# Forget block, attention keys, gates and branches computed by feature in a transformer block on one core

## What is computed

```python
h = rms_norm(x, pre_mix_norm[l])
proj = h @ w_in[l]
(hq, hf, hi, hg, mq, mk, mv, dq, dkv, iq, ik, iw, gates) = jnp.split(proj, splits, axis=-1)
y_a = hgrn2_mixer(hq, hf, hi, hg, lower_bounds[l], hg_norm_w[l])     # f = lb + (1-lb) sigmoid(hf)
y_b = moba_attention(mq, mk, mv, bias_b)
y_c = dsa_attention(dq, c_kv, w_uk, w_uv, iq, ik_n, iw, bias_c, n_keep)
g = jax.nn.sigmoid(gates.reshape(B, S, N_BRANCH, D_MODEL))
merged = (g[:, :, 0] * (y_a @ w_branch_a[l])
          + g[:, :, 1] * (y_b @ w_branch_b[l])
          + g[:, :, 2] * (y_c @ w_branch_c[l]))
x = x + rms_norm(merged @ w_out[l], post_mix_norm[l])
h2 = rms_norm(x, pre_ffn_norm[l])
gate, up = jnp.split(h2 @ w_ffn_in[l], 2, axis=-1)
x = x + rms_norm((jax.nn.silu(gate) * up) @ w_ffn_out[l], post_ffn_norm[l])
```

## Time and profile before

| | before |
|---|---|
| median of 3 runs | 463.78 us (463.74 to 463.91) |
| the profiled execution's own time | 463.29 us |
| its span, first to last instruction | 461.6 us |
| granted TensorE clock, share of full speed | 0.999 |
| TensorE busy | 454.1 us (98%), 3318 matmuls |
| VectorE busy | 301.5 us (65%) |
| ScalarE busy | 248.9 us (54%) |
| GpSimd busy | 49.1 us (11%) |

### The profile page before, as it was taken

One profiled execution on the slowest core, in us unless ns is written; L12 is line 12 of the kernel. 1 busy time (PEld: TensorE's weight loads), 2 busy tenths in 40 slices (PEclk: granted clock), 3 DMA queues, 4 the chain that ended last, 5 costly groups with the idle time before them and its releaser, 6 DMA issues.

```text
span 461.6 us, 8038 instructions
## 1 busy us (share of the span) xinstructions
PE 454.1 (98%) x3318; PEld 400.3 (87%) x3318; DVE 301.5 (65%) x403; ACT 248.9 (54%) x370; POOL 49.1 (11%) x50
## 2 busy tenths in 40 slices
PE   8999999999999999999999999999999999999994
PEld 7799798987788888888888888999999999888883
DVE  4657689898628746577449797866565665743532
ACT  5768369338485955526443462855544554433410
POOL 2301002456630100000000000100000000000000
PEclk9999999999999999999999999999999999999999
DMA  8997665545434464569565544666666656766202
GB/s 296 398 296 221 187 172 179 173 130 159 148 125 135 140 183 136 184 186 322 190 210 186 184 168 148 216 192 189 188 191 207 192 187 188 247 200 186 89 0 91
DMA packets 26024, 85.60 MB, mean 185 GB/s; under 512 B 3171, under 2 KB 4740, under 8 KB 25988
## 3 DMA queue, kind: packets, MB, share of 16 engines
q1 hardware_dynamic: 25268, 84.31, 57.4%
q10 hardware_dynamic: 720, 0.79, 0.5%
HBM read 83.84 MB, written 1.25 MB: 184 GB/s over the span
## 4 chain that ended last, share of the span: by engine, by line
PE 97%; DVE 1%; DMA 1%; SPq 0%; ACT 0%; issue 0%; DVEq 0%
PE bank L1450 56%; PE bank L1444 31%; PE bank L1476 1%; PE bank L1620 1%; PE bank L1485 1%; DMA raw<-w_stream 1%; PE bank L1632 1%; PE bank L1660 1%; PE bank L1604 1%; PE bank L1584 1%; PE bank L1575 1%; PE bank L1521 1%; PE bank L1523 0%; PE bank L1526 0%; PE bank L1633 0%; PE bank L1664 0%
## 5 line engine op out<-in xcount | busy, mean ns | idle before, releaser
L843 DVE TENSOR_TENSOR wl<-raw,wh 128x1024 fp32r<-128x1024 f32 (+1 forms) x150 | 185.0, 1267 | 44.3 <-ACT wh L514 44.0
L514 ACT ACTIVATE wh<-raw 128x1024 fp32r<-128x1024 f32 (+1 forms) x150 | 153.5, 1049 | 83.7 <-PE bank L1450 42.0
L1444 PE MATMUL bank<-hTh,wh 128*128 128x256 f32 x416 | 116.2, 279 | 0.0
L1444 PE MATMUL bank<-hTl,wh 128*128 128x256 f32 x416 | 115.1, 277 | 0.0
L1444 PE MATMUL bank<-hTh,wl 128*128 128x256 f32 x416 | 115.1, 277 | 0.0
L1450 PE MATMUL bank<-wh,hTh 128*128 128x512 f32 (+1 forms) x216 | 85.4, 395 | 0.2 <-DVE wl L843 0.2
L1450 PE MATMUL bank<-wh,hTl 128*128 128x512 f32 (+1 forms) x216 | 83.0, 384 | 0.0
L1450 PE MATMUL bank<-wl,hTh 128*128 128x512 f32 (+1 forms) x216 | 83.0, 384 | 0.0
L1444 PEld LDWEIGHTS bank<-hTh,wh 128*128 128x128 f32 x416 | 78.1, 188 | 0.5 <-issue 0.3
L1444 PEld LDWEIGHTS bank<-hTh,wl 128*128 128x128 f32 x416 | 78.2, 188 | 0.1
L1444 PEld LDWEIGHTS bank<-hTl,wh 128*128 128x128 f32 x416 | 78.2, 188 | 0.0
(11 more groups left out here) (227 smaller groups left out, 528.7 us busy)
## 6 DMA issues: line engine op xcount, KB each, us to landing
raw<-w_stream SPq DMA_DIRECT2D x146, 512.0 KB, 4.1
raw<-w_stream SPq DMA_DIRECT2D x4, 328.0 KB, 6.5
x<-x_in SPq DMA_DIRECT2D x4, 256.0 KB, 4.2
raw<-w_stream SPq DMA_DIRECT2D x4, 256.0 KB, 4.3
bias<-bias_scratch SPq DMA_DIRECT2D x8, 128.0 KB, 4.8
x<-x_in SPq DMA_DIRECT2D x1, 1024.0 KB, 5.7
out<-mo SPq DMA_DIRECT2D x3, 256.0 KB, 2.0
post<-post_mix ACTq DMA_DIRECT2D x1, 512.0 KB, 9.8
```

Of the source, the lines that this page charges most:

```text
L514: did(act.activation(wh[:, u % SPLIT, place(u)], raw[:, u % RING, place(u)], ACT.Copy), high_done, u + 1 - EARLY)
L843: did(dve.tensor_tensor(wl[:, u % RING, place(u)], raw[:, u % RING, place(u)], wh[:, u % SPLIT, place(u)].bitcast(F32), ALU.subtract), low ...
L1444: ins = pe.matmul(bank[bk][:, i * S:(i + 1) * S], w_[:, k, h * P:(h + 1) * P], x_[:, kt, :], start=first, stop=final, skip_group_check=True)
```

## The change

Fourteen blocks are made by feature in place of by token: `hf`, `mk`, the six gate and the six branch blocks. Their transposes (`hfT`, `mkT`, `mTa`, `mTb`) go. A new job `row1` makes the factors of the first norm a row, from `qp` (which holds ones at that time) and a diagonal that VectorE writes; ScalarE copies it to `row1`. `by_token` on VectorE multiplies PSUM by that row for `hf`, `mk` and the gates. ScalarE then applies its sigmoids in SBUF. `merged` is kept by feature, and its high and low halves (`mTh`, `mTl`) are written straight from it. `SHIFT` becomes 32 floats, 128 bytes, so all stationary units, those of the feed-forward layer too, move by 64 bytes in their slots.

```diff
 CHUNKS = DFF // 512
-BY_FEATURE = ("dq", "hq", "mq") + tuple(f"f{c}{j}" for c in "gu" for j in range(CHUNKS))
+BY_FEATURE = ("dq", "hf", "hq", "mq", "mk") + tuple(f"{n}{b}{c}" for n in ("gate", "branch") for b in BRANCHES for c in range(2)) + tuple(f"f{c}{j}" for c in "gu" for j in range(CHUNKS))
 SHIFTED = BY_FEATURE + ("uk",)
-SHIFT, PLACE = 16, 1024 + 64
+SHIFT, PLACE = 32, 1024 + 64
...
 N_MASKS = len(IN_STRIP) * HALF_STRIP
-JOBS = (["hT00", "hT10", "hT01", "hT11", "rel", "ckvT", "iqT0", "iqT1", "kc0", "kc1", "vc0", "vc1", "ikT"]
-        + [f"ix{i}" for i in range(6)] + ["hfT0", "hfT1",
+JOBS = (["hT00", "hT10", "hT01", "hT11", "rel", "ckvT", "iqT0", "iqT1", "row1", "kc0", "kc1", "vc0", "vc1", "ikT"]
+        + [f"ix{i}" for i in range(6)] + [
                                           "diag", "L1", "dl0", "dl1", "dl2", "L2", "L4", "L8", "L16",
-                                          "mkT0", "mkT1", "mkT2", "mkT3", "L32", "dP0", "dP1", "dP2", "dP3", "L64", "dO0", "dO1", "L128",
+                                          "L32", "dP0", "dP1", "dP2", "dP3", "L64", "dO0", "dO1", "L128",
                                           "ml0", "ml1", "ml2", "ho0", "ho1", "mP0", "mP1", "mP2", "mP3",
                                           "mO0", "mO1", "yaT0", "yaT1", "yaT2", "yaT3",
-                                          "mTa0", "mTa1", "mTa2", "mTa3", "mTb0", "mTb1", "mTb2", "mTb3", "h2T00", "h2T01", "h2T10", "h2T11",
+                                          "h2T00", "h2T01", "h2T10", "h2T11",
                                           "row", "fT"])
...
         sig = sb("sig", [P, 3, TT, 512])
-        skip = [sb("skip0", [P, SHIFT])]
+        row1 = sb("row1", [P, S])
+        skip = [sb("skip0", [P, 16])]
         yh = [sb(f"yh{b}", [P, H, S], F32R) for b in range(3)]
...
         iws = sb("iws", [P, TT, NI], stack=early)
-        skip.append(sb("skip1", [P, SHIFT], stack=early))
+        skip.append(sb("skip1", [P, 16], stack=early))
         ckvT = sb("ckvT", [P, RT, S], stack=early)
...
         row2 = row.rearrange("p (o s) -> p o s", o=1).to_broadcast([P, 2, S])
+        diag1 = prob[:, 0:S]
+        rows1 = row1[:].rearrange("p (o s) -> p o s", o=1).to_broadcast([P, 2, S])
+        merged2 = merged[:].rearrange("p t d -> p (t d)").rearrange("p (c t n) -> p c t n", c=2, t=TT)
...
             o_sums one_exp out_mean out_rstd out_squares out_sums prob_ready relu_used score_ready
-            silu_last silu_done row_diag fT_low fgu_high down_eps stored x1_ready x1_squares x_rstd x_squares y_high
+            silu_last silu_done row_diag row1_diag row1_ready gate_sig mT_low fT_low fgu_high down_eps stored x1_ready x1_squares x_rstd x_squares y_high
         """.split()
...
             copy_jobs(["iqT1"], lambda i: flat(iqT, 1))
+            ps = wait_job(act, "row1")
+            did(act.activation(row1[:], ps[:, 0:S], ACT.Copy), *job_read("row1"))
             high_until(17)
...
                 did(act.activation(relu[:, i % 2], ps[:, 0:512], ACT.Relu, scale=DI ** -0.5), *job_read(f"ix{i}"))
-            stage_copy("hf", 0, 512, 21)
-            high_until(22)
-
             high_until(24)
             for i in range(2):
-                ps = wait_job(act, f"hfT{i}")
-                did(act.activation(flat(pre, i), ps[:, 0:512], ACT.Sigmoid))
-                did(act.activation(flat(kT, i), ps[:, 0:512], ACT.Sigmoid, scale=-1.0), *job_read(f"hfT{i}"))
+                act.wait_ge(*block_read("hf", i))
+                did(act.activation(flat(pre, i), stage[:, 0, i], ACT.Sigmoid))
+                did(act.activation(flat(kT, i), stage[:, 0, i], ACT.Sigmoid, scale=-1.0))
             act.wait_ge(lb_ready, 1)
...
             normalise(0)
-            stage_copy("mk", 0, 512, LAST_UNIT["mk"] + 5)
-            high_until(40)
-            for r in range(NSTRIP):
-                ps = wait_job(act, f"mkT{r}")
-                did(act.activation(token_strip(kcT, r), strip_bank(ps), ACT.Copy), *job_read(f"mkT{r}"))
             high_until(41)
...
                 name = f"gate{b}{c}"
-                high_until(LAST_UNIT[name] + 4)
-                if c:
-                    after_block(act, f"branch{b}0")
+                high_until(LAST_UNIT[name] + 5)
                 for t in range(TT):
-                    ps = wait_block(act, name, t)
-                    did(act.activation(sig[:, b, t], ps[:, 0:512], ACT.Sigmoid, scale=stat(X_RS + t)), *block_read(name, t))
+                    act.wait_ge(*block_read(name, t))
+                    did(act.activation(sig[:, b, t], sig[:, b, t], ACT.Sigmoid), s["gate_sig"], TT * (3 * c + i) + t + 1)
...
             probT_copy("m")
-            gates(1, 0)
+            high_until(52)
             y_high(["mO0", "mO1"], 1, 1)
...
                 did(act.activation(token_strip(yh[0], r), strip_bank(ps), ACT.Copy), s["y_high"], 5 + r)
+            gates(1, 0)
             gates(2, 0)
             high_until(FIRST_UNIT[f"gate{BRANCHES[0]}1"] + 5)
+
             def m_high(c):
-                for r in range(NSTRIP):
-                    ps = wait_job(act, f"mT{'ab'[c]}{r}")
-                    did(act.activation(token_strip(mTh, r, 4 * c, 4), strip_bank(ps), ACT.Copy), s["mT_high"], 4 * c + r + 1)
+
+                for t in range(TT):
+                    act.wait_ge(s["merged"], 4 * c + TT + t + 1)
+                    did(act.activation(f_tiles(mTh, c, t), pair(merged2[:, c, t]), ACT.Copy), s["mT_high"], TT * c + t + 1)
...
                     s["ckv_ready"], t + 1)
+            for t in range(TT):
+                dve.wait_ge(eye_made, 1)
+                did(dve.tensor_scalar(diag1[:, t * P:(t + 1) * P], eye[:], stat(X_RS + t), None, ALU.mult), s["row1_diag"], t + 1)
             low_until(11)
...
+            def by_token(name, dst):
+
+                for t in range(TT):
+                    ps = wait_block(dve, name, t)
+                    did(dve.tensor_tensor(pair(dst(t)), pair(ps[:]), rows1, ALU.mult), *block_read(name, t))
+
             for i in range(6):
+                if i == 4:
+                    after_job(dve, "row1")
+                    by_token("hf", lambda t: stage[:, 0, t])
                 add_heads(i)
...
             low_until(37)
+            by_token("mk", lambda t: flat(kcT, t))
             level(4)
...
                         did(ins)
+            def gate_rows(i, c):
+
+                b = BRANCHES[i]
+                by_token(f"gate{b}{c}", lambda t: sig[:, b, t])
+
+            low_until(49)
+            gate_rows(0, 0)
             low_until(52)
+            gate_rows(1, 0)
             y_low(["mO0", "mO1"], 1, 1)
...
                     low_until(LAST_UNIT[f"branch{b}{c}"] + 3)
-                    after_block(dve, f"gate{b}{c}")
+                    dve.wait_ge(s["gate_sig"], TT * (3 * c + i + 1))
                     for t in range(TT):
                         ps = wait_block(dve, f"branch{b}{c}", t)
-                        dst = merged[:, t, c * 512:(c + 1) * 512]
+                        dst = merged2[:, c, t]
                         out_ = dst if i == 0 else tmp[:, t]
...
                         for t in range(TT):
-                            dst = merged[:, t, c * 512:(c + 1) * 512]
+                            dst = merged2[:, c, t]
                             n_merged[0] += 1
...
             def m_low(c):
-                for r in range(NSTRIP):
-                    ps = wait_job(dve, f"mT{'ab'[c]}{r}")
-                    dve.wait_ge(s["mT_high"], 4 * c + r + 1)
-                    did(dve.tensor_tensor(token_strip(mTl, r, 4 * c, 4), strip_bank(ps), token_strip(mTh, r, 4 * c, 4).bitcast(F32), ALU.subtract),
-                        *job_read(f"mT{'ab'[c]}{r}"))
-
+                for t in range(TT):
+                    dve.wait_ge(s["mT_high"], TT * c + t + 1)
+                    did(dve.tensor_tensor(f_tiles(mTl, c, t), pair(merged2[:, c, t]), f_tiles(mTh, c, t).bitcast(F32), ALU.subtract), s["mT_low"], TT * c + t + 1)
+
+            low_until(LAST_UNIT[f"gate{BRANCHES[2]}0"] + 4)
+            gate_rows(2, 0)
             merge(0)
...
             m_low(0)
+            for i in range(3):
+                low_until(LAST_UNIT[f"gate{BRANCHES[i]}1"] + 4)
+                gate_rows(i, 1)
             merge(1)
...
                             h = 2 * t + i
-                            for w_, x_ in ((rh, hTh), (rl, hTh), (rh, hTl)):
-                                first = kt == i == 0 and w_ is rh and x_ is hTh
-                                final = kt == n_kt - 1 and x_ is hTl
+                            for w_, x_ in ((rh, high), (rl, high), (rh, low)):
+                                first = kt == i == 0 and w_ is rh and x_ is high
+                                final = kt == n_kt - 1 and x_ is low
                                 ins = pe.matmul(bank[bk][:, i * S:(i + 1) * S], w_[:, k, h * P:(h + 1) * P], x_[:, kt, :], start=first, stop=final,
...
             transposes("iqT1", tiles(stage[:, 1], 0))
```

(21 more changed lines are left out.)

## The result

The changed kernel takes 472.06 us (median, 471.77 to 472.11) against 463.78 us before: ratio 1.0175, 95% interval 1.0164 to 1.0186. It is slower by 8.3 us, where 3.9 us less was forecast. The rival that the shift makes the slow pace the rule is what happened. Single executions far above the others of their kernel (925.12 us in e2, 504.85 in e13, 1610.17 in e14, 1174.98 and 1616.57 in the kernel before) are left out of all that follows.

What follows compares the result with a forecast made beforehand. The prediction took TensorE's own instruction stream as the bound: 463.29 us - 3.43 + 0.35 + 0 - 0.77 gave 459.4, as a median 459.9 us. The forecast's own range was 459.3 to 460.6, the wider range 459.2 to 463.2.

Steps and rivals of the forecast that it cites:

- The rival that the shift makes the slow pace the rule: Every by-feature unit: 0.11 us more for each slow one, 470.5 us with all 96 slow; chance 0.18.
- TensorE's stream is the time: Whole kernel: TensorE busy 98% of 461.6 us, 97% of the chain, its products waiting 0.2 us for a weight unit.
- Four transposition groups, 3.43 us, less row1's 0.35: TensorE loses the hfT, mkT, mTa and mTb transposes, 3.43 us, and gains the row1 product, 0.35 us.
- 528 matmuls turned into 1056 at no cost: hf, mk, gate and branch blocks: two by-feature matmuls at 113.3 ns cost one by-token at 226.7, so 0.
- Shifted: 64 to 128 bytes, "I take the fast end": All by-feature units at their new place: none slow any more, seven slow ones gained back, - 0.77 us.
- The other end: Same shift of the stationary units: all 96 by-feature units slow, 9.8 us more.
- The rival that the shift does nothing: By-feature units: slow ones stay and restarts are drawn as before, 461.4 us or 462.7 us; chance 0.20.
- VectorE and ScalarE moves at nothing: Norm multiplications for hf, mk and gates, and sigmoids in SBUF: covered by time to spare, cost 0.
- a late engine: Rival: VectorE or ScalarE late, the copy of the transposed probabilities first, 1 to 3 us back, 461 to 463; chance 0.07.

Runs made afterwards that it cites:

- e2: Kernel before with its stationary weights moved to 128 bytes, nothing else changed; 469.46, 471.4 and 471.63 us.
- e13: Changed kernel with the high halves of the weights at 64 bytes and the low halves at 192; 460.09 us, ratio 0.9912 to 0.9955.
- e14: Changed kernel with its stationary weights at 64 bytes and one gate unit alone at 192; 462.68 us, ratio to the kernel before 0.9987.
- e16: Kernel before with the high halves of the weights at 64 bytes and the low halves at 192; 463.04 us, ratio 0.9978 to 1.0001.
- e15: Changed kernel with high halves of the weights at 64 bytes and low halves at 192, a repeat of e13; 460.35 us, ratio 0.9929.
- e11: Kernel before with only its stationary weights moved to 128 bytes, a repeat of e2 for its profile; 469.65 us.
- e1: Changed kernel with its stationary weights back at 64 bytes, all else kept; 464.91 us, ratio to the kernel before 1.0024.
- e7: Changed kernel with its stationary weights at 64 bytes and the token operands also moved by 64 bytes; 479.16 us, ratio to the kernel before 1.0325.
- e9: Changed kernel with its stationary weights at 64 bytes, but at 192 from the third gate to the last branch; 464.95 us, ratio 1.0030.
- e10: Changed kernel with its stationary weights at 64 bytes in even units and at 192 in odd units; 461.62 us, ratio 0.9952.
- e12: Changed kernel with each by-feature unit's first k-tile at 64 bytes and its second at 192; 460.19 us, ratio 0.9941.

## Why the prediction was wrong, point by point

- *TensorE's stream is the time.* Right: 98% busy, the same chain, the same waits. The 0.2 us of waiting for weights left out the 0.3 us at the start, which both kernels have.
- *Four transposition groups, 3.43 us, less row1's 0.35.* Right. The pauses are gone, row1 costs 0.36, and e16 less e15 gives 2.7 for the net 3.1.
- *528 matmuls turned into 1056 at no cost.* Right at the held pace: 26 gate and branch units at 113.3 ns in e15, where before 226.7 was taken by token. The Trainium skill ("TensorE: Matmul & The Clock Gate", section "Back-to-back issue gap") gives N/2.4 + 2.5 ns as the gap of an isolated matmul, a condition that the prediction left out when it held the rule against a stream. The 2.5 ns show here as little as in the earlier trace rows.
- *Shifted: 64 to 128 bytes, "I take the fast end".* This step failed. Its ground was that 45 of 52 by-feature units were fast, but those were 45 units at 64 bytes, in few stretches that keep what they draw; they said nothing of 128 bytes. The other end, which the working had (all 96 slow), was the case, and even that was a little low: 118.7 to 120 ns instead of 117.9, 0.13 a unit instead of 0.11, so 472.06 instead of the rival's 470.5. The term was - 0.77 us; measured, it is 12.4 less 0.77, + 11.6. With that the sum is 463.29 - 3.08 + 11.6 = 471.8, and the profiled execution took 471.77. e11 shows that the shift alone does it: 6.1 us on the old kernel.
- *The rival that the shift does nothing* had its price too low. At 64 bytes (e1) the change has 464.9, not 461.4 to 462.7: 50 slow units, not 13 or 25. The long stretch from u51 on, which it named, did start slow, and the gate blocks ahead of it too. The prediction took from the Trainium skill ("SBUF — State Buffer", section "Who interferes with whom": two independent read ports, shared with nobody) that a place could not matter. The runs disagree: between e7 with 120.0 ns and e1 with 113.3 or 117.8 only the token operands, and the tensors behind them, were moved.
- *VectorE and ScalarE moves at nothing; a late engine.* Right: TensorE waits nowhere that it didn't wait in the kernel before. That holds in e15 too, where its products run at 113.3 ns and leave the other engines less time.

What stays open: why the distance between the two operands sets the pace, and whether it is their reads that disturb each other; why a restart begins fast or slow at 64 and 192 bytes (e1, e9 and e14 have the same places up to u49, and u49 runs at 118 ns in e1 and e14 and at 113 in e9); and why a step away and back moves a stretch to the fast pace while none was seen to move one to the slow pace. In e10, e12 and e14 no stretch turned at a step from 64 to 192. One step from 192 to 64 can be enough, as at u52 in e10, behind a unit that itself started at 192; it was not enough at u30 and u32. The runs show that it is so and not by what.

## What to carry to other kernels

A unit's address is part of its price: before taking a pace over to another place or another form, find a row at that place, and count stretches between pauses, not units, when judging how often a pace occurs. When a change moves the time by a few per cent and no engine waits, compare the start-to-start distance of the main matmul before and after in a block that the change was not meant to touch; here the feed-forward blocks told it in two rows. Where the stationary operand is the streamed one, letting its high and low parts lie 64 bytes to either side of the moving operand's place (modulo 256) gave 460.35 us against 463.04 for the old form with the same places and 463.58 for the kernel before.

## What the hardware showed that was not expected

- The pace of a 256-column matmul depends on the distance between weights and token columns modulo 256 bytes: 120.0 ns at 0, 118.7 (in places 120) at 128, 117.3 to 118.7 in the long stretches at 32 and 96, 113.3 or 117.8 at 64 and 192.
- A 512-column matmul with the token tile stationary has 226.7 ns at distance 0 and 233.4 ns with its token tile 64 bytes off: the two forms want different places.
- At 64 bytes a stretch that starts at 117.8 stays so over 27 units, u51 to u77 (e1), but one unit at 192 bytes turned it to 113.3 at the step back to 64 (e14). The same step turned the slow stretches of e12 and some of e10 (u20, u52), but not u30 and u32 of e10. Stretches at 113.3 stayed there through every change of place.
